# First scores ahead of the linear attention's output, a later transposition of MIX, and value products over two query tiles

## The reference, cut to what matters

```
o_gla  = silu(g) * rms_norm(o_f + o_b)              # 4 heads of 64, gated linear attention, both directions
o_fnet = real(fft2(u)) @ w_mix                      # 256 features
s = (q_nope . k_nope + q_rope . k_rope) * scale     # 8 heads, 512 queries x 512 keys, 96 features
o_mla  = softmax(s) @ v                             # 8 heads of 64
x = x + concat[o_gla, o_fnet, o_mla] @ w_out
x = x + hier_moe(rms_norm(x))                       # 32 experts, 3 MB of weights each
```

## Time and profile before

| what | value |
|---|---|
| median of 3 runs | 569.71 us (569.33 to 574.26) |
| profiled execution | 573.0 us, span 571.2 us |
| PE, DVE, ACT, POOL busy | 498.0, 215.4, 145.4, 91.8 us |
| PE busy, share | 87% |
| mean granted clock of PE | 0.948 |
| read from memory | 131.49 MB |

### The profile page before, as it was taken

How to read it: one execution, slowest core, us unless ns; L and a number is a source line. 1 busy time by engine, 2 the same in 40 slices (tenths; PEclk the granted TensorE clock), 3 DMA queues, 4 the chain that set the end, 5 groups by cost and what they waited for, 6 DMA issues and landing times. The chain is left out here.

```text
span 571.2 us, 7521 instructions
## 1 busy us (share of the span) xinstructions
PE 498.0 (87%) x2864; PEld 276.6 (48%) x2864; DVE 215.4 (38%) x529; ACT 145.4 (25%) x337; POOL 91.8 (16%) x104
## 2 busy tenths in 40 slices
PE   4999999997799998999989799999999987877600
PEld 3455544584556665444547455545554544433200
DVE  3237111828467663013863322223222330221157
ACT  4314102427256763121212111111111110110112
POOL 1000002472010000000212023322322231211100
PEclk9999999999979998999996999999999998999855
DMA  8960000100079502900158899999999999999573
GB/s 285 327 182 0 2 1 4 44 0 2 0 279 417 225 1 83 390 28 16 39 196 320 292 415 417 416 416 415 418 413 415 417 416 416 417 416 407 207 293 148
DMA packets 38261, 137.03 MB, mean 240 GB/s; under 512 B 9830, under 2 KB 12966, under 8 KB 30032
## 3 DMA queue, kind: packets, MB, share of 16 engines
q1 hardware_dynamic: 33152, 128.38, 57.2%
q0 software_dynamic: 4976, 8.11, 4.0%
q10 hardware_dynamic: 96, 0.03, 0.0%
HBM read 131.49 MB, written 12.72 MB: 252 GB/s over the span
## 5 line engine op out<-in xcount | busy, mean ns | idle before, releaser
L964 PE MATMUL bank<-EW,WO 128*64 128x256 f32 x640 | 77.3, 396 | 11.0 <-DMA EW<-in_moe_w_up 10.3
L1741 POOL DMA_INDIRECT y_scratch<-G,sidx x32 | 39.2, 1225 | 172.1 <-DVE G L1576 156.2
L687 PE MATMUL bank<-EW,XT 128*128 128x512 f32 (+1 forms) x192 | 64.1, 495 | 0.0
L964 PEld LDWEIGHTS bank<-EW,WO 128*64 128x64 f32 x640 | 46.4, 143 | 35.7 <-DMA EW<-in_moe_w_up 11.5
L890 PE MATMUL bank<-WO,XT 128*128 128x512 f32 x128 | 58.0, 610 | 1.0 <-DVE XT L1462 1.0
L1233 ACT ACTIVATE G<-bank 128x128 f32<-128x128 f32 x32 | 8.9, 278 | 183.5 <-PE bank L964 183.5
L1563 DVE TENSOR_TENSOR G<-G,bank 128x128 f32<-128x128 f32 x32 | 9.2, 288 | 106.7 <-ACT G L1233 104.5
L687 PEld LDWEIGHTS bank<-EW,XT 128*128 128x128 f32 x192 | 32.9, 190 | 31.0 <-issue 31.0
L1576 DVE COPY G<-bank 128x512 f32<-128x512 f32 x32 | 22.1, 692 | 58.1 <-PE bank L977 58.1
L977 PE MATMUL bank<-EW,G 128*64 128x512 f32 x160 | 38.6, 603 | 0.8 <-issue 0.8
L890 PEld LDWEIGHTS bank<-WO,XT 128*128 128x128 f32 x128 | 24.4, 195 | 30.3 <-issue 30.3
(11 more groups left out here) (269 smaller groups left out, 650.0 us busy)
## 6 DMA issues: line engine op xcount, KB each, us to landing
EW<-in_moe_w_gate SPq DMA_DIRECT2D x20, 1024.0 KB
EW<-in_moe_w_up SPq DMA_DIRECT2D x20, 1024.0 KB
EW<-in_moe_w_down SPq DMA_DIRECT2D x20, 1024.0 KB, 23.7
WO<-in_w_out SPq DMA_DIRECT2D x2, 2048.0 KB, 12.3
MIX<-in_moe_w_gate SPq DMA_DIRECT2D x4, 1024.0 KB, 24.3
MIX<-in_moe_w_up SPq DMA_DIRECT2D x4, 1024.0 KB, 23.7
WO<-in_moe_w_gate SPq DMA_DIRECT2D x4, 1024.0 KB
WO<-in_moe_w_up SPq DMA_DIRECT2D x4, 1024.0 KB
```

The source lines that it names most:

```text
L687: mm = pe.matmul(ps[:, 0:width], xnT[:, c, t * P:(t + 1) * P], w_in_sb[:, c, col:col + width], start=(c == 0), stop=(c == C - 1))
L964: mm = pe.matmul(bank[BLOCK * m:BLOCK * (m + 1), 0:2 * P].rearrange("p (w n) -> p w n", w=2), xeT[:, buf, c, par * BLOCK:(par + 1) * BLOCK ...
L1741: pool.indirect_dma_start(y_rows, bass.IndirectOffsetOnAxis(ap=sidx[:, e:e + 1], axis=0), Y[:, e % 2], None, bounds_check=4 * S - 1, oob_i ...
```

## The change

1. Scores 0 to 2, with their maxima and exponentials, move on PE, DVE and ACT to before the tiles "o". On DVE, the normalising of items 0 to 2 stands between the sums of squares of those tiles. The tiles "o" go to banks 4 to 7.
2. The four transpositions of MIX move from step 2 to step 8.
3. The items are ordered anew: item i is heads pair i // 8, query half i // 4 % 2, tile i // 2 % 2, head u = i % 2. One AV takes four items, two tiles at once: the same 16 instructions, each over 256 columns, at steps 8, 12, ..., 36. There are 8 of them, not 16. A bank O holds two heads over all 512 queries.
4. `probsT` becomes two buffers of four items, twice the size, and lies in place 3 of EW. The load of expert 3's gate and up weights so moves behind the reading of the O tiles, ahead of those for experts 0 and 1.

```diff
@@ psum_plan
+    for i in range(EARLY):                 # EARLY, MIX_TURN = 3, 8
+        use(("S", i), i % 3)
+    turn[0] = 4
     for t in range(T):
         ring(("o", t))
...
-        elif i % 4 == 0:
-            use(("O", i // 4), 6 + i // 4 % 2, fill=0)
+        elif i % 2 == 0:
+            use(("O", i // 2), 6 + i // 2 % 2, fill=0)
@@ attention_order
-        if i == 2:
+        if i == MIX_TURN:
             steps += [("mT", c) for c in range(4)]
-        if i >= 6 and i % 2 == 0:
-            steps.append(("AV", (i - 6) // 2))
+        if i >= 8 and i % 4 == 0:
+            steps.append(("AV", (i - 8) // 4))
+def attention_item(i):
+    pair, half, tile, u = i // 8, i // 4 % 2, i // 2 % 2, i % 2
+    return 2 * half + tile, 2 * pair + u, i // 4 % 2, tile, u
@@
-        probsT = view(G, 2048, (4, S))
+        probsT = view(ew23, 6144, (2, 2, T, 2 * P))
@@ SP
-            for s in (2, 3):
-                load_gate_up(s, s)
-                load_down(s, s)
+            load_gate_up(2, 2)
+            load_down(2, 2)
+            load_down(3, 3)
             for c in range(4):
                 drained(sp, ("mT", c))
             load_gate_up(RING, RING)
             for t in range(T):
                 drained(sp, ("O", t))
+            load_gate_up(3, 3)
@@ PE, before the tiles "o"
+            for i in range(EARLY):
+                scores(i)
@@ PE, AV
-                    drained(pe, ("PT", 2 * i))
-                    drained(pe, ("PT", 2 * i + 1))
+                    for j in range(4 * i, 4 * i + 4):
+                        drained(pe, ("PT", j))
                     for kc in range(T):
                         for u in range(2):
                             h = 2 * hp + u
-                            mm = pe.matmul(ps_o[MV * u:MV * (u + 1), hp * P:(hp + 1) * P],
-                                           V[:, kc, h * MV:(h + 1) * MV],
-                                           probsT[:, (2 * i + u) % 4, kc * P:(kc + 1) * P],
+                            mm = pe.matmul(ps_o[MV * u:MV * (u + 1), half * 256:(half + 1) * 256],
+                                           V[:, kc, h * MV:(h + 1) * MV], probsT[:, i % 2, u, kc, :],
@@ ACT
+            for i in range(EARLY):
+                exponent(i)
             for t in range(T):
                 ps = filled(act, ("o", t))
                 act.activation(osq[:, t], ps[:, 0:GH * GDV], ACT.Square).then_inc(squares_ready, 1)
...
-                    if j >= 4:
-                        act.wait_ge(av_done, (j - 4) // 2 + 1)
+                    if j >= 8:
+                        act.wait_ge(av_done, j // 4 - 1)
@@ DVE
+            for i in range(EARLY):
+                row_max(i)
             for t in range(T):
                 dve.wait_ge(squares_ready, T + 8 + t + 1)
                 link(dve.tensor_reduce(rgla[:, 3, t * GH:(t + 1) * GH], ...))
+                if t >= 1:
+                    normalise(t - 1)
...
-                    dve.wait_ge(av_done, (tq + 1) * 4)
-                    free_bank(dve.tensor_copy(xnT[:, 4:8, tq * P:(tq + 1) * P],
-                                              ps[:, :].rearrange("p (c n) -> p c n", c=4)), ("O", tq))
+                    dve.wait_ge(av_done, 2 * tq + 2)
+                    free_bank(dve.tensor_copy(xnT[:, 4 + tq, :], ps[:, :]), ("O", tq))
```

More of the change, by code:

```diff
@@ L57 @@
 PAIRS = NE // 2
+EARLY, MIX_TURN = 3, 8
 OVB = S // BLOCK
@@ L127, in psum_plan @@
         if kind == "S":
-            use(("S", i), i % 3)
+            if i >= EARLY:
+                use(("S", i), i % 3)
         elif kind == "mT":
@@ L814, in _, with scores @@
                 close_bank(mm, ("qT", h))
+            def scores(i):
+                ps = open_bank(("S", i))
+                tq, h = attention_item(i)[0:2]
+                close_bank(pe.matmul(ps[:, :], qT[0:QD, h, tq * P:(tq + 1) * P], kT[0:QD, h, :],
+                                     start=True, stop=True), ("S", i))
+            pe.wait_ge(krope_copied, 16 * (MH - 1))
+            for h in range(0, MH, 2):
+                drained(pe, ("kT", h))
+            for h in range(2):
+                drained(pe, ("qT", h))
+            for i in range(EARLY):
+                scores(i)
             pe.wait_ge(state_diag_ready, 2 * GH)
@@ L831, in _ @@
                 close_bank(mm, ("o", t))
-            pe.wait_ge(krope_copied, 16 * (MH - 1))
-            for h in range(0, MH, 2):
-                drained(pe, ("kT", h))
             for h in range(MH):
@@ L862, in _ @@
                 else:
-                    tq, hp = i // 4, i % 4
-                    if hp == 0:
-                        ps_o = open_bank(("O", tq))
-                    drained(pe, ("PT", 2 * i))
-                    drained(pe, ("PT", 2 * i + 1))
+                    hp, half = i // 2, i % 2
+                    if half == 0:
+                        ps_o = open_bank(("O", hp))
+                    for j in range(4 * i, 4 * i + 4):
+                        drained(pe, ("PT", j))
                     for kc in range(T):
@@ L1164, in _, with exponent @@
                 free_bank(act.activation(qT[0:QD, h, :], ps[0:QD, :], ACT.Copy), ("qT", h))
+            def exponent(i):
+                ps = filled(act, ("S", i))
+                act.wait_ge(neg_max, i + 1)
+                if i >= 4:
+                    act.wait_ge(bank_full[PLAN[("PT", i - 4)][0]], PLAN[("PT", i - 4)][1])
+                free_bank(act.activation(probs[:, i % 4], ps[:, :], ACT.Exp, bias=nm[:, i:i + 1],
+                                         accum_out=rs[:, i:i + 1]), ("S", i))
+            for i in range(EARLY):
+                exponent(i)
             for t in range(T):
@@ L1171, in _ @@
             for i in range(T * MH + 3):
[L1172 to L1179, removed]
+                if EARLY <= i < T * MH:
+                    exponent(i)
+                if i == MIX_TURN:
                     for c in range(0, 4, 2):
@@ L1185, in _ @@
                     ps = filled(act, ("PT", j))
-                    if j >= 4:
-                        act.wait_ge(av_done, (j - 4) // 2 + 1)
-                    free_bank(act.activation(probsT[:, j % 4], ps[:, :], ACT.Copy), ("PT", j))
+                    if j >= 8:
+                        act.wait_ge(av_done, j // 4 - 1)
+                    _, _, g, tile, u = attention_item(j)
+                    free_bank(act.activation(probsT[:, g, u, :, tile * P:(tile + 1) * P],
+                                             ps[:, :].rearrange("p (k n) -> p k n", k=T), ACT.Copy), ("PT", j))
             for step in OUT_ORDER:
@@ L1428, in _, with row_max, normalise @@
                 free_bank(dve.tensor_copy(qT[0:QD, h, :], ps[0:QD, :]), ("qT", h))
+            def row_max(i):
+                ps = filled(dve, ("S", i))
+                dve.tensor_reduce(nm[:, i:i + 1], ps[:, :], AX, ALU.max, negate=True).then_inc(neg_max, 1)
+            def normalise(i):
+                drained(dve, ("S", i))
+                link(dve.reciprocal(ri[:, i:i + 1], rs[:, i:i + 1]))
+                dve.tensor_scalar(probs[:, i % 4], probs[:, i % 4], ri[:, i:i + 1], None, ALU.mult).then_inc(norm_ready, 1)
+            for i in range(EARLY):
+                row_max(i)
             for t in range(T):
@@ L1441, in _ @@
                                             ALU.mult), ("o", t))
[L1443 to L1446, removed]
             for i in range(T * MH + 6):
[L1449 to L1452, removed]
+                if EARLY <= i < T * MH:
+                    row_max(i)
+                if EARLY < i <= T * MH:
                     normalise(i - 1)
-                if i == 2:
+                if i == MIX_TURN:
                     for c in range(1, 4, 2):
```

## The result

Over 15 runs each the median fell from 570.55 to 567.07 us; the ratio, an estimate from all the runs and not the quotient of the two medians (that is 0.9939), is 0.9916, 95% interval [0.9889, 0.9943], so about 4.8 us (3.3 to 6.3). The profiled execution took 568.71 us, its span is 566.8 against 571.2. The forecast of 567.0 and its range held.

What follows compares the result with a forecast made beforehand. Experts bound by weight transfers that PE releases, so the output product's start decides: 3.0 + 2.0 - 1.8 - 0.5 = 2.7 us earlier (1.0 to 4.5). From the median 569.71 that gives 567.0 (565.2 to 568.7); range with rivals 562.5 to 571.5.

Steps and rivals of the forecast that it cites:

- The frame: Weights' transfers bound the experts and PE releases them, so an earlier output product (before at 224.41) makes the end equally earlier.
- Opening: From the tiles "o" to scores 9: scores 9 start at 171.5 where they started at 174.48, a gain of 3.0 us.
- The chain to MIX: In the opening, DVE writes MIX from 158.4 to 159.9, and PE waits some 1.4 us for PT 1.
- ACT needs just as much ... together 1.30: Attention's steady part: ACT needs 0.68 exponential to copy plus 0.62 to the next exponential, as much as PE's 1.30 an item.
- POOL beside DVE: POOL's product of MIX runs while DVE normalises items 3 and 4: a loss of 0.5 us, bounds 0 and 0.8.
- The product: One AV over two tiles takes 1.87 us, 2.02 with its neighbours; bounds for the product 1.71 and 2.04.
- Scores 9 to 31: Stretch from scores 9 to scores 31 takes 39.5 us where it took 41.5: a gain of 2.0.
- The end: Scores 31 to the output product takes 10.2 us where it took 8.44, with waits before two long products: loss 1.8.
- ACT and DVE keep up: Faster rival, chance 0.17: in the opening only the 1.4 us MIX wait stays; gain 7.3 in all, time 562.4.
- The rival: Slower rival, chance 0.13: PE's clock falls in the new opening behind four idle times of about 1 us; time 571.3.
- hidden by the transfers: No-effect rival, chance 0.10: the expert weight stream has its own time and the gain goes into its slack; 569.7.
- Two smaller signs: Expected in PE's trace: waits over 1 us on ACT's copy before each of the last two products; second mT waits for ACT's copy.

## Why the prediction was right

**The frame held.** The first reload and the end moved by the same amount (4.28 and 4.4), so the question was the output product's start. That start is at 221.84, within the 221 to 222 that were forecast, but by luck: 2.23 of slow clock and late start ahead of the stretch stand against the 2.1 by which the gain was forecast too small. Counted from the first scores it is 4.80 earlier.

**Opening.** Forecast 3.0, less 0.5 for POOL: 2.5. Measured 3.67. The chain to MIX came as written: PE waited 1.11 where 1.4 was forecast, scores 3 followed at once, the second mT waited for ACT's copy. The step that was mis-sized is "ACT needs just as much ... together 1.30". ACT needs 1.16, DVE 1.19, and so the pace behind the MIX write is DVE's 1.19. In the steady part before, both wait for PE's 1.30: the exponential waits for DVE's maximum, and the maximum for the scores. In the earlier trace rows no idle time is printed there, and I took the spacing of starts for the engine's own cost. Over the four steps from exponential 3 to exponential 7 this is about 0.4, and about 0.3 more since the MIX write ended and exponential 3 came that much earlier than forecast. The last three mT cost 1.46 and not 1.75, another 0.3, as the clock was whole (before, the first of them ran slow). Some 0.1 more is in the product and its neighbours.

**POOL beside DVE.** Forecast 0.5 between 0 and 0.8; the instruction grew by 0.71 and the path by 0.63. The rule of the Trainium skill (SBUF — State Buffer, Who interferes with whom), that whoever starts first keeps the shared ports to its end, gave 0.7 from the forecast's times. The trace agrees with its direction, DVE issued second and was held: the normalising started 0.92 before POOL's recorded end and took 0.71 longer. The row of before, which had such a wait only on POOL's side, was rightly read as a nearly full one. The upper end was the better value.

**The product.** Forecast 1.87, measured 1.88; a period without other waits is 7.22 (170.67 to 177.89), as forecast. The gate and up products' row, same shape and other operands, was the right one to price by.

**Scores 9 to 31.** Forecast 2.0, measured 2.40: the two waits where DVE copies a finished bank are 0.18 each and not 0.4. At 1.19 an item DVE and ACT get back about 0.1 of the copy's delay in each of the following items, which the forecast at 1.30 left out.

**The end.** Forecast a loss of 1.8, measured 1.28: waits of 0.97 and 0.88 for 1.25 and about 1.3. Place and cause were right. Of the 0.5, 0.1 is that exponential 30 was earlier (1.03 behind scores 31 for 1.16); most of the rest is the product with the step behind it, 1.87 for 2.05, and the last three copies up to the last product, 2.42 for 2.6.

The three differences, 1.17, 0.40 and 0.52, make the 2.1 us between 2.7 and 4.80. The one misreading, 1.30 for 1.19, accounts for about 0.9 of it (0.4, 0.4 and 0.1), somewhat under half. With 4.80 in place of 2.7 the forecast from 569.71 would have been 564.9. That the time was met to 0.1 us is luck for the most part: the three runs of before had their median at 569.71 and fifteen had it at 570.55, and the two medians of fifteen are 3.5 apart where ratio and stretch say 4.8.

**The rivals.** That ACT and DVE keep up (gain 7.3) was half right: they are faster than forecast, but PE still waits for them at scores 6, at the next transposed item and at two mT, and 4.80 lies between 2.7 and 7.3. The clock didn't fall in the new opening in any of the seven profiles with scores ahead and MIX at step 8, 12 or the end, where PE idles 1.7 to 2.7 us in about ten; it fell in all three with one long wait, 3.94, 3.95 and 5.93. The rival spoke of the new opening, though, and a fall did come ahead of it. Nothing was hidden by the transfers. Two smaller signs missed their mark: the waits before the last two products are 0.97 and 0.88 and not over 1, and the first mT waited too (0.41), not only the second.

## What to carry to other kernels

The spacing of starts on an engine is its cost only where nothing else can set it: before calling an engine full, look whether each start coincides with the end of its input, also where no idle time is printed. When a wait is removed ask who made it: here a chain over DVE and ACT stayed as late as it was, and the gain was what PE could do meanwhile, so a step that depends on that chain must be moved behind it (step 3 or step 8 decided all of the gain). Fixed work without a deadline, such as the transpositions of MIX, is best kept for the waits at a stage's end, where it cost nothing.

## What the runs showed of the hardware

**The clock differs between executions of the same stretch by more than this change is worth.** From the output product to the first reload PE runs the same instructions in all kernels, and they took from 85.53 to 93.59 us. The stretch 304 to 306, about the same place, of the change and of the kernel with MIX at step 12 (busy PE, PEld, DVE, ACT, POOL, clock, DMA share, GB/s):

```profile
304.00:306.00 2.00, 2.00 (x12) 2.00 (x11) 0.42 (x4) 1.14 (x4) 0.50 (x1) 0.50 0.96 355
```

```profile
304.00:306.00 2.00, 2.00 (x22) 1.31 (x20) 0.35 (x2) 0.00 (x0) 0.07 (x1) 1.00 1.11 300
```

In the change PE's clock was at 1.2 GHz from about 299 to 313, in the other it was whole from 290 to 314. Over the whole part from output product to first reload the clock was at 0.50 for 17.1 us before, 13.7 in the change and with POOL's product cut, 6.8 in four kernels, 3.4 in two and 0 with MIX at step 12, and the times follow: 93.59, about 91.9, 88.7 to 88.9, 87.0 to 87.2, 85.53, so about half of the slow time is lost. The 2.55 us wait ahead of the linear attention's scores is another such place: the clock stayed whole behind it before and with wide products only, and fell in the other eight profiles, for 1.6 to 2.9 us of PE's time; those eight are the ones with scores ahead, as said above. The output product started slow before and in none of the nine others, among them one with the same three idle times ahead of it. What decides between the two in one execution isn't settled by these runs.

**A product of POOL stretches a DVE scalar operation on SBUF from 0.49 to 1.20 us** and leaves a maximum out of PSUM beside it as it is (two in 1.28 with either size of POOL's product). The stretched row, 1.19 or 1.20, is in all six profiles with POOL's product whole and MIX behind step 3. The wait stands in the DVE row's length: no idle time is printed for it.
